# Latent attention's projections with tokens on partitions, woven between the mLSTM's panels, and the heads' gating moved into the attention

## The chip, the core and the metric
One core of a Trainium2 chip runs one program. It has a matrix engine (TensorE, PE below), a vector engine (DVE), a scalar engine (ACT), GpSimd (POOL) and a queue engine (SP) that here only issues weight loads. The metric is the time of one execution in device microseconds; the kernel before has a median of 2100.88 us over 3 runs (2096.22 to 2100.93).

## What is computed
Two transformer blocks follow one another over 512 tokens of width 1024. The change is in the second block's mixer, which the reference writes so:
```python
proj = h @ w_in
u, v_m, o_pre, i_pre, f_pre, c_q, c_kv, k_r = split(proj)
u_c = silu(causal_dwconv(u, conv_w, conv_b))
q_m, k_m = u_h @ wq_m, u_h @ wk_m            # per head, 128 -> 64
hm = mlstm_chunkwise(q_m, k_m, v_h, ig, fg)
y_m = sigmoid(o_pre) * rmsnorm(hm)
q_a = rmsnorm(c_q) @ w_uq                    # 4 heads x (128 + 64)
kv = rmsnorm(c_kv) @ w_ukv                   # 4 heads x (128 + 128)
q_rope = apply_rope(rmsnorm(q_a[rope part]), cos, sin); q_nope = rmsnorm(rest)
k_rope = apply_rope(rmsnorm(k_r), cos, sin); k_nope = rmsnorm(kv[first part])
o_a = causal_block_attention(q, k, v);  y_a = rmsnorm(o_a)
return concat([y_m, y_a]) @ w_out
```
A first MLP stands before it, and a cross attention over 256 memory rows and a second MLP behind it.

## The kernel before, in words
Activations lie with features on partitions: `h_hi`, `h_lo` hold the normalised input as a high and a low part, and each product with weights is three products of fp32r operands (high with high, low with high, high with low). Weights come in panels. SP loads panel n into one of two raw slots, POOL splits it into `w_hi` and `w_lo` (lines 2563 and 2568, four pieces each), and may begin when PE has finished panel n-2, because the split buffers too have two slots. PE multiplies panels in the order in which `Linear` objects are made. A block of 512 results goes into one of four PSUM banks (`banks[blk % 4]`); PE may start block n when block n-4 has been read (`acc_free`).

`pe_panel` (line 393) multiplies with features on the output's partitions; `pe_panel_tokens` (line 439) with tokens there, two token tiles in one bank. `mlstm_pe` takes the gates' panel `L_if`, the two panels of u, two of v and two of the output gate by tokens, and turns the gate rows on the way (line 1863). DVE convolves each block of u (`mlstm_conv_dve`), then computes the gates' rows with four partitions in use (lines 1978 to 1991) and the rope angles. ACT waits for the gates before it reads v. Then come the q and k products, and the four heads: a broadcast (line 1911), Exp on ACT, scores (line 1886), their weighting on DVE (line 2009), values (line 1897) and division (line 2022).

`latent_pe`, `latent_act` and `latent_dve` do the latent attention's preparation after that, with features on partitions. c_q is projected behind the heads and c_kv behind that. Every RMS norm needs a sum over partitions: ACT squares a block, PE forms the sums with one-column products (line 2132), ACT and DVE take roots and inverses, PE spreads them into rows (line 2143), DVE multiplies (line 2151). V is turned to tokens by PE (line 2187). Rope's swaps are ACT copies, its products for q DVE and, at the end, POOL (`rope_pool`, lines 2348 to 2351), which stands in POOL's queue behind the splits of the first two output panels. Then `attn_pe`, `attn_act` and `attn_dve` run 16 units (4 heads by 4 query tiles): scores (line 1339), the masked minimum (line 1418), Exp (line 1385), transposes (line 1349), copy (line 1393), values (line 1363), result (line 1429). The output projection follows, with its mLSTM half first.

Of the kernel before, what the change touches and what calls it, by code (L numbers as in the profile page):

```python
# [20 lines left out]
F32 = mybir.dt.float32  # L21
# [6 lines left out]
P = 128  # L28
# [31 lines left out]
def build_program(nc, io, out):  # L60
    ctx = ExitStack()
    with ctx:
# [31 lines left out]
        cols = sb("cols", [P, 584])  # L94
# [47 lines left out]
        for k in range(CONV2):  # L142
# [15 lines left out]
        col_at["qr"], col_at["kr"] = ncol, ncol + 1  # L158
        part_loads = [(64, ncol, io["qk_norm_q_2"][:, NOPE:A_QK].rearrange("o p -> p o")),
                      (64, ncol + 1, io["qk_norm_k_2"][:, NOPE:A_QK].rearrange("o p -> p o"))]  # L160
        ncol += 2
        inv = io["rope_inv"].rearrange("(p o) -> p o", o=1)
        col_at["inv"] = ncol
        part_loads += [(64, ncol, inv), (96, ncol, inv)]
        ncol += 1
        col_at["ib"], col_at["fb"] = ncol, ncol + 1
        part_loads += [(0, ncol, io["b_igate_2"].rearrange("o h -> h o")), (0, ncol + 1, io["b_fgate_2"].rearrange("o h -> h o"))]
# [13 lines left out]
        ncol += 64  # L181
        col_at["neg_sink"] = ncol
# [115 lines left out]
        L_if = Linear(1, DB, 132, [0, 4], lambda i: w_in2[:, :, IF0:IF0 + 132])  # L298
        L_m = [Linear(2, DB, 256, [0, 128], column_panels(w_in2, c0, 2)) for c0 in (0, 512, 1024)]
        L_qm = Linear(1, 4, 64, [], lambda i: io["wq_m_2"][0].rearrange("h p e -> p h e"))  # L300
        L_km = Linear(1, 4, 64, [], lambda i: io["wk_m_2"][0].rearrange("h p e -> p h e"))
        for L in (L_qm, L_km):
            L.nb = 4
            Linear.blocks += 4
        L_km.b0 = L_qm.b0 + 4
        L_cq = Linear(1, DB, 256, [0, 128], lambda i: w_in2[:, :, CQ0:CQ0 + 256])
        L_ckv = Linear(1, DB, 256, [64, 128], lambda i: w_in2[:, :, IN2 - 256:IN2])
        uq_offs = [o for h in range(A_HEADS) for o in (A_QK * h, A_QK * h + 64)]
        L_uq = Linear(1, 2, 768, uq_offs, lambda i: rows_of(io["w_uq_2"][0]))
        L_ukv = Linear(1, 1, 1024, [128 * j for j in range(8)], lambda i: rows_of(io["w_ukv_2"][0]))  # L310
# [13 lines left out]
        const_loaded = sem("const_loaded")  # L324
        const_made = sem("const_made")
# [15 lines left out]
        def last_block(panel):  # L341
            for L in Linear.made:
                if L.p0 <= panel < L.p0 + L.n:
                    if L in (L_uq, L_ukv):
                        return L_uq.b0 + 16
                    return L.b0 + (panel - L.p0 + 1) * L.nb
            raise ValueError(panel)
# [140 lines left out]
        def act_to_features(act, dst, d0, nb, gain, tiles, ring=banks[4:8]):  # L488
            for b in range(nb):
# [7 lines left out]
        def dve_to_features(dve, dst, d0, nb, gain, tiles, ring=banks[4:8]):  # L497
            for b in range(nb):
# [1152 lines left out]
        def mix_act(act):  # L1651
# [4 lines left out]
            act.dma_start(XAGAIN, x_in).then_inc(x_loaded, 16)  # L1656
            preload(act, ACT.Sqrt)
# [50 lines left out]
        def mlp_act(act, k):  # L1708
            for half in range(2):
# [16 lines left out]
                if half == 0 and k == 0:  # L1726
                    act_evac(act, L2, lambda b: YA[:, b, :])
                if half == 1 and k == 0:
# [6 lines left out]
        def mlp_dve(dve, k):  # L1735
            for half in range(2):
# [9 lines left out]
                for b in range(16):  # L1746
# [5 lines left out]
                    low(b)  # L1752
                if half or k:
# [23 lines left out]

        o = 0
        QM = A(o, 1024).rearrange("p (b s) -> p b s", b=2); o += 1024
        KM = A(o, 1024).rearrange("p (b s) -> p b s", b=2); o += 1024
        RING = [A(o, 512), A(o + 512, 512)]; o += 1024
        EW = A(o, 1280); o += 1280

        ROW = [r[0:4, :] for r in (a_free_hi[:, 12, :], a_free_hi[:, 15, :], EW[:, 0:512], A(o, 512), EW[:, 512:1024], A(0, 512), A(1024, 512))]
        o = 5120

# [918 lines left out]
```

## Time and profile before
| | |
|---|---|
| Median of 3 runs | 2100.88 us |
| The profiled execution's own time, and its span | 2111.39 us, 2109.7 us |
| PE busy in the span | 1988.1 us (94%) |
| POOL | 1543.9 us (73%) |
| DVE | 890.7 us (42%) |
| ACT | 654.3 us (31%) |
| Mean granted clock of PE | 0.957 |
| Chain that ended last | PE 77%, POOL 12%, DVE 6% |

### The profile page before, as it was taken

Reading aid. Unit: us, or ns where it says so; the run is one execution under the profiler, and the core shown is the slowest. Engines: PE = TensorE matmul, PEld = TensorE weight load, DVE = VectorE, ACT = ScalarE, POOL = GpSimd, SP = SyncE. Lnnn points to the kernel's source line nnn. Section 1 sums busy time; section 2 is a strip of 40 time slices with the busy share of each in tenths; the row PEclk is TensorE's granted clock in tenths of the full one; section 3 lists DMA queues with packets and bytes.
Section 4 is the critical chain, followed back from the end, with each engine's and each line's share of the span. In section 5 each row is a group of like instructions: output and inputs, shape, how many; then the busy total and the mean of one; then the engine's idle time right before and its main releaser. Section 6 shows DMA issues by size and latency. Waiting matters only on the chain.

```text
span 2109.7 us, 26714 instructions
## 1 busy us (share of the span) xinstructions
PE 1988.1 (94%) x9907; PEld 1664.1 (79%) x9907; DVE 890.7 (42%) x1703; ACT 654.3 (31%) x1216; POOL 1543.9 (73%) x1379
## 2 busy tenths in 40 slices
PE   6999999999999999889999989889898889999998
PEld 4888888887878888778888877868667777888887
DVE  4566767641025435274014227742444055402421
ACT  4466666542035661132012002432231142200200
POOL 7799989797844449789889888633609809988985
PEclk9999999999999999999999999987698899999999
DMA  6222222123332222313332332201102302333232
GB/s 216 81 61 61 61 60 61 60 60 100 90 99 73 61 79 84 116 60 100 100 98 88 94 89 63 66 26 60 40 1 80 101 20 80 100 100 100 89 96 74
DMA packets 212124, 166.01 MB, mean 79 GB/s; under 512 B 13439, under 2 KB 208322, under 8 KB 211635
## 3 DMA queue, kind: packets, MB, share of 16 engines
q1 hardware_dynamic: 207126, 147.61, 23.6%
q10 hardware_dynamic: 4892, 17.01, 2.3%
q8 instruction: 64, 1.05, 0.2%
q14 instruction: 42, 0.34, 0.1%
HBM read 161.43 MB, written 7.37 MB: 80 GB/s over the span
## 4 chain that ended last, share of the span: by engine, by line
PE 77%; POOL 12%; DVE 6%; issue 2%; ACT 2%; DMA 0%; DVEq 0%; SPq 0%; ACTq 0%; POOLq 0%
PE bank L393 55%; POOL w_lo L2568 5%; POOL w_hi L2563 4%; PE bank L439 4%; PE bank L1363 3%; PE bank L1339 3%; PE bank L412 2%; PE bank L2132 1%; PE bank L1349 1%; PE bank L2239 1%; POOL arena L1056 1%; PE bank L1038 1%; DVE arena L1816 1%; PE bank L1016 1%; PE bank L485 1%
## 5 line engine op out<-in xcount | busy, mean ns | idle before, releaser
L2563 POOL TENSOR_TENSOR w_hi<-w_raw,one 128x512 fp32r<-128x512 f32 (+2 forms) x520 | 532.8, 1055 | 492.8 <-PE bank L393 415.2
L2568 POOL TENSOR_TENSOR w_lo<-w_raw,w_hi 128x512 fp32r<-128x512 f32 (+2 forms) x600 | 742.7, 1269 | 34.6 <-ACT w_hi L1201 30.2
L393 PE MATMUL bank<-h_hi,w_hi 128*128 128x512 f32 (+1 forms) x1096 | 436.9, 399 | 15.5 <-POOL w_lo L2568 8.1
L393 PE MATMUL bank<-h_hi,w_lo 128*128 128x512 f32 (+1 forms) x1096 | 426.0, 389 | 0.0
L393 PE MATMUL bank<-h_lo,w_hi 128*128 128x512 f32 (+1 forms) x1096 | 424.8, 388 | 0.0
L393 PE MATMUL bank<-a_hi,w_hi 128*128 128x512 f32 x848 | 332.7, 392 | 11.2 <-POOL w_lo L2568 6.7
L393 PE MATMUL bank<-a_hi,w_lo 128*128 128x512 f32 x848 | 331.9, 391 | 0.0
L393 PE MATMUL bank<-a_lo,w_hi 128*128 128x512 f32 x848 | 331.6, 391 | 0.0
L393 PEld LDWEIGHTS bank<-h_hi,w_hi 128*128 128x128 f32 x1096 | 209.8, 191 | 57.3 <-POOL w_lo L2568 9.2
L393 PEld LDWEIGHTS bank<-h_hi,w_lo 128*128 128x128 f32 x1096 | 209.2, 191 | 42.6
L393 PEld LDWEIGHTS bank<-h_lo,w_hi 128*128 128x128 f32 x1096 | 210.1, 192 | 36.9
L393 PEld LDWEIGHTS bank<-a_hi,w_hi 128*128 128x128 f32 x848 | 160.6, 189 | 46.0 <-POOL w_lo L2568 7.6
L393 PEld LDWEIGHTS bank<-a_hi,w_lo 128*128 128x128 f32 x848 | 160.2, 189 | 33.8
L393 PEld LDWEIGHTS bank<-a_lo,w_hi 128*128 128x128 f32 x848 | 160.5, 189 | 33.1
L1742 DVE TENSOR_TENSOR a_lo<-arena,a_hi 128x512 fp32r<-128x512 f32 x64 | 80.4, 1256 | 158.0 <-ACT a_hi L1714 158.0
L1722 ACT ACTIVATE arena<-bank 128x512 f32<-128x512 f32 x64 | 38.1, 596 | 323.2 <-PE bank L393 315.0
L439 PE MATMUL bank<-w_hi,h_hi 128*128 128x256 f32 x384 | 111.3, 290 | 7.1 <-ACT arena L1844 6.6
L439 PE MATMUL bank<-w_lo,h_hi 128*128 128x256 f32 x384 | 109.7, 286 | 0.0
L439 PE MATMUL bank<-w_hi,h_lo 128*128 128x256 f32 x384 | 109.7, 286 | 0.0
L923 DVE SCALAR_TENSOR_TENSOR arena<-bank,cols,arena 128x510 f32<-128x510 f32 (+1 forms) x128 | 95.5, 748 | 4.8 <-ACT arena L907 1.4
L1750 DVE TENSOR_TENSOR arena<-arena,bank 128x512 f32<-128x512 f32 x64 | 43.2, 675 | 99.1 <-ACT arena L1722 92.4
L439 PEld LDWEIGHTS bank<-w_hi,h_hi 128*128 128x128 f32 x384 | 74.8, 195 | 7.8 <-issue 6.8
(387 smaller groups left out, 2924.6 us busy)
## 6 DMA issues: line engine op xcount, KB each, us to landing
w_raw<-in_w_in SPq DMA_DIRECT2D x32, 1024.0 KB, 5.3
w_raw<-in_w_ff SPq DMA_DIRECT2D x32, 1024.0 KB, 5.4
w_raw<-in_w_mlp_in SPq DMA_DIRECT2D x16, 1024.0 KB, 5.3
w_raw<-in_w_mlp_out SPq DMA_DIRECT2D x16, 1024.0 KB, 5.8
w_raw<-in_w_in SPq DMA_DIRECT2D x25, 512.0 KB, 4.3
w_raw<-in_w_ssd_out SPq DMA_DIRECT2D x8, 1024.0 KB, 5.6
bias_rows<-bias_row ACTq DMA_DIRECT2D x1, 4096.0 KB, 16.1
w_raw<-in_w_attn_out SPq DMA_DIRECT2D x4, 1024.0 KB, 5.3
```

What stands on the lines that cost most here:

```text
L393: mm = pe.matmul(bank[:, 0:ntok], a, b[:, koff + k, 0:ntok], start=(k == 0 and n == 0), stop=(k == L.kb - 1 and n == 2))
L412: mm = pe.matmul(banks[blk % 4][:], a, b[:, koff + k, :], start=(k == 0 and n == 0), stop=(k == L.kb - 1 and n == 2))
L439: mm = pe.matmul(banks[blk % 4][:, t * L.w:(t + 1) * L.w], a[:, k, tok], b, start=(k == 0 and n == 0), stop=(k == L.kb - 1 and n == 2))
L485: mm = pe.transpose(ring[b % len(ring)][:, t * P:(t + 1) * P], src[:, t, b * P:(b + 1) * P], ident[:])
L923: ins = dve.scalar_tensor_tensor(dst[:, lo:hi], src[:, lo + s:hi + s], colv(f"conv_w{k}", conv_column(g, b)), dst[:, lo:hi], ALU.mult, ALU ...
L1339: mm = pe.matmul(score_bank[n % 2][:, 0:w["n"]], qT, kT, start=(i == 0), stop=(i == len(w["q"]) - 1))
L1363: mm = pe.matmul(value_bank[:, 0:dv], mem[1][n % 2][:, j * P:(j + 1) * P], w["v"][j], start=(j == 0), stop=(j == nb - 1))
L1722: act.activation(RL[b % 2], acc(L1, b), ACT.Relu).then_inc(ml_relu, 1)
L1742: dve.tensor_tensor(a_lo[:, b, :], SQR[b % 2], a_hi[:, b, :].bitcast(F32), ALU.subtract).then_inc(ml_lo, 1)
L1750: dve_link(dve.tensor_tensor(RL[b % 2], RL[b % 2], NROW[:], ALU.mult))
L2563: pool.tensor_tensor(w_hi[:, slot, part], raw[:, slot, part], one[:].broadcast_to([P, n]), ALU.mult).then_inc(split_hi, 1)
L2568: ins = pool.tensor_tensor(w_lo[:, slot, part], raw[:, slot, part], w_hi[:, slot, part].bitcast(F32), ALU.subtract)
```

## The change
- Panels are reordered: u (2 panels), gates (one block; i in the first 64 columns, f in the next), c_q, c_kv with k_r (192 columns), q and k of the mLSTM in one panel of 128 columns per head, v (2), q up, gate panel, k and v up, gate panel. c_q, c_kv and the two up projections are now multiplied with tokens on partitions, so their norms are sums along the free axis (ACT's Square with a running sum, or DVE reductions), and their results are turned by transposes on PE (16 for c_q, c_kv and k_r, 40 for q and k). V needs none. The one-column sums and the spread rows of this stage go.
- Rope tables are made with tokens on partitions (128 columns in place of 512) during the first MLP; POOL multiplies the gains in (12 products), ahead of the third panel's split. Rotation is done by DVE. `rope_pool` goes.
- The conv's split of block b is issued after the conv of block b+1. q and k of the mLSTM are copied by ACT instead of DVE.
- The latent attention starts right behind the mLSTM heads. The gating of the heads' outputs by the output gate, their transposes and splits are hooks in its units.
- The load of the saved memory features is issued when the attention starts. Six small loads (gains, positions) are issued by ACT before the output projection of the first mixer.

```diff
-        L_if = Linear(1, DB, 132, [0, 4], lambda i: w_in2[:, :, IF0:IF0 + 132])
-        L_m = [Linear(2, DB, 256, [0, 128], column_panels(w_in2, c0, 2)) for c0 in (0, 512, 1024)]
...
+        L_u = Linear(2, DB, 256, [0, 128], column_panels(w_in2, 0, 2))
+        L_if = Linear(1, DB, P, [0], lambda i: [w_in2[:, :, c:c + 64] for c in (IF0, IF0 + M_HEADS)])
         L_cq = Linear(1, DB, 256, [0, 128], lambda i: w_in2[:, :, CQ0:CQ0 + 256])
+        L_ckv = Linear(1, DB, 192, [0, 64], lambda i: w_in2[:, :, CKV0:IN2])
+        L_qk = Linear(1, M_HEADS, P, [0] * M_HEADS, lambda i: [io[w][0].rearrange("h p e -> p h e") for w in ("wq_m_2", "wk_m_2")])
+        L_v = Linear(2, DB, 256, [0, 128], column_panels(w_in2, 512, 2))
+        L_uq = Linear(1, 2, 768, [0] * 2 * T, lambda i: rows_of(io["w_uq_2"][0]))
+        L_gate_m = [Linear(1, DB, 256, [0, 128], column_panels(w_in2, 1024, 1))]
+        L_ukv = Linear(1, 1, 1024, [0] * 2 * T, lambda i: rows_of(io["w_ukv_2"][0]))
+        L_gate_m.append(Linear(1, DB, 256, [0, 128], column_panels(w_in2, 1280, 1)))
...
         def mlstm_pe(pe):
+            pe_panel_rows(pe, L_u, 0, h_x, normed("mix2"))
+            pe_panel_with_root(pe, L_u, 1)
+            pe_panel(pe, L_if, 0, 0, h_x)
+            pe_panel_tokens(pe, L_cq, 0, 0, h_x)
+            pe_panel_tokens(pe, L_ckv, 0, 0, h_x)
+
+            pe.wait_ge(sp_lo, 4)
...
+            pe_panel_tokens(pe, L_v, 0, 0, h_x)
+            pe_panel_tokens(pe, L_v, 1, 1, h_x, only=0)
+            pe.wait_ge(lt["low"], 1)
...
+            pe_panel_tokens(pe, L_v, 1, 1, h_x, only=1)
...
+            for i in range(2 * T):
+                up_pe(pe, L_uq, i, 8, 384)
+            pe_panel_tokens(pe, L_gate_m[0], 0, 0, h_x)
+            pe.wait_ge(split_ready, L_ukv.p0 + 1)
+            for i in range(2 * T):
+                up_pe(pe, L_ukv, i, 10, 512)
+            pe.wait_ge(ml["act"], 4)
+            for f in range(6):
+                turn_pe(pe, f)
+            pe_panel_tokens(pe, L_gate_m[1], 0, 0, h_x)
+            for f in range(6, 10):
+                turn_pe(pe, f)
             mlstm_bc_pe(pe, 0)
...
+        def low_rank_act(act):
+
+            tokens_act(act, L_cq, 0, lambda t: CQT[:, t, :])
+            tokens_act(act, L_ckv, 0, lambda t: CKT[:, t, :])
...
+        def q_block_act(act, i):
+            t, j = i // 2, i % 2
+            bank = acc(L_uq, i, 0, P, 384)
+            act.wait_ge(acc_ready, L_uq.b0 + i + 1)
+            act.activation(QT[t][:, j * 384:(j + 1) * 384], bank, ACT.Copy)
+            if i >= 2:
+                act.wait_ge(lt["red"], i - 1)
+            act.activation(SQUARES[i % 2][:, 0:384], bank, ACT.Square).then_inc(acc_free, 1)
...
+        HEAD_AT = {"scale": 2, "turn": 4, "hi": 5, "lo": 6}
 
         def latent_pe(pe):
...
+            first = tp_n["pe"]
+            hooks = {HEAD_AT["turn"] + h: [lambda h=h: pe_to_features(pe, OM, T, h + 1, OM_RING, counted(ml["head"], 0), first=h)] for h in range(4)}
+            pe.wait_ge(ml["out"], 4 * M_HEADS)
+            attn_pe(pe, latent_units(), AMEM, hooks)
+            pe.wait_ge(tp_free, first + 4)
             for b in range(4):
                 pe_panel(pe, L_out2, b // 2, b // 2, a_x, only=b % 2, ks=range(0, 4))
...
-                if panel == L_out2.p0 + 2:
-                    rope_pool(pool)
```

## Rows read from the trace of the kernel before
**Rows 1.** The page: PE's line of section 1, clock in 40 slices.
```profile
PE 1988.1 (94%) x9907; PEld 1664.1 (79%) x9907; DVE 890.7 (42%) x1703; ACT 654.3 (31%) x1216; POOL 1543.9 (73%) x1379
...
PEclk9999999999999999999999999987698899999999
```
**Rows 2.** Table of stretches; columns in its first line.
```profile
core 0: us, PE busy (x) PEld busy (x) DVE busy (x) ACT busy (x) POOL busy (x), PEclk, DMA share, GB/s
...
1295.50:1364.00 68.50, 60.86 (x442) 58.15 (x440) 52.92 (x54) 17.34 (x29) 49.49 (x40) 0.95 0.22 66
1364.00:1410.20 46.20, 40.03 (x146) 27.35 (x144) 24.67 (x71) 20.64 (x66) 20.00 (x24) 0.78 0.16 52
...
1458.00:1486.00 28.00, 28.00 (x100) 23.80 (x99) 4.75 (x7) 3.60 (x8) 0.00 (x0) 0.51 0.00 1
...
1515.20:1537.00 21.80, 21.80 (x54) 10.25 (x54) 5.48 (x26) 5.83 (x18) 11.01 (x9) 0.61 0.03 9
1537.00:1561.70 24.70, 23.32 (x130) 15.36 (x130) 13.84 (x67) 11.78 (x31) 0.00 (x0) 1.00 0.00 0
```
**Rows 3.** Timeline, PE: start, us, instruction, [idle before, releaser].
```profile
1337.13 0.55 PE L439 MATMUL bank<-w_hi,h_hi 128*128 128x256 f32 x1 [6.63 <-ACT arena L1844]
...
1515.20 0.46 PE L1339 MATMUL bank<-a_free_lo,a_free_hi 128*128 128x128 f32 x2 [3.21 <-POOL arena L2351]
...
1561.74 0.47 PE L393 MATMUL bank<-a_hi,w_hi 128*128 128x512 f32 x1
```
**Rows 4.** Chain of work in time (start, us, what), and one timeline row, PE.
```profile
1352.44 11.70 PE bank L439 x96
...
1410.24 11.19 PE bank L393 x48
...
1572.76 1.91 PE L485 MATMUL bank<-ident,arena 128*128 128x128 f32 x16
```
**Rows 5.** Timeline, POOL: one split of a full panel.
```profile
1295.93 4.81 POOL L2563 TENSOR_TENSOR w_hi<-w_raw,one 128x512 fp32r<-128x512 f32 x4 [1.89 <-PE bank L393]
1300.70 6.38 POOL L2568 TENSOR_TENSOR w_lo<-w_raw,w_hi 128x512 fp32r<-128x512 f32 x4
```
**Rows 6.** Timeline, DVE: conv's start, the gate chain and two of its operations.
```profile
1296.24 0.69 DVE L1811 TENSOR_TENSOR a_free_hi<-bank,a_free_lo 128x512 f32<-128x512 f32 x1
...
1332.15 1.52 DVE L1978 SCALAR_TENSOR_TENSOR arena<-a_free_hi 4x512 f32<-4x512 f32 x1
...
1338.70 1.65 DVE L809 TENSOR_TENSOR arena<-arena 4x512 f32<-4x512 f32 x1
...
1343.76 0.68 DVE L811 TENSOR_TENSOR arena<-arena 4x512 f32<-4x512 f32 x1
...
1350.53 0.41 DVE L1991 TENSOR_SCALAR arena<-arena 4x512 f32<-4x512 f32 x1
```
**Rows 7.** Timeline, ACT: table load, first Exp of the heads, Square, copies.
```profile
1351.69 1.28 ACT L1847 ACT_TABLE_LOAD   x1
...
1370.08 0.40 ACT L1927 ACTIVATE arena<-a_free_lo,small 128x128 f32<-128x128 f32 x1
...
1382.21 0.29 ACT L1955 ACTIVATE a_free_lo<-arena 128x128 f32<-128x128 f32 x1
...
1448.81 1.08 ACT L2280 ACTIVATE arena<-bank 64x512 f32<-64x512 f32 x2
```
**Rows 8.** Timeline, PE and DVE: first score and last scaling of the heads.
```profile
1371.98 0.69 PE L1886 MATMUL bank<-arena 64*128 64x512 f32 x1 [1.10 <-DVE arena L2001]
...
1409.58 1.13 DVE L2022 TENSOR_SCALAR arena<-bank,small 128x128 f32<-128x128 f32 x4
```
**Rows 9.** Timeline, PE: scores of the attention at full clock.
```profile
1535.10 1.02 PE L1339 MATMUL bank<-a_free_lo,a_free_hi 128*128 128x512 f32 x2
...
1538.17 0.39 PE L1339 MATMUL bank<-a_free_lo,a_free_hi 128*128 128x128 f32 x2
...
1547.19 0.28 PE L1339 MATMUL bank<-a_free_lo,a_free_hi 128*128 128x128 f32 x1
```

More of the change, by code:

```diff
@@ L1752, in mlp_dve @@
                     low(b)
+                if half == 0 and k == 0:
+                    rope_tables_dve(dve)
                 if half or k:
@@ new lines, in turned_bank, with turn_pe @@
+        def turned_bank(f):
+            return banks[4 + f % 4] if f < 6 else banks[4 + (f - 6) % 3]
+        def turn_pe(pe, f):
+            if f >= 4:
+                pe.wait_ge(lt["kept"], 6 if 6 <= f < 9 else f - 2 if f == 9 else f - 3)
+            bank = turned_bank(f)
+            if f < 4:
+                pe.wait_ge(lt["qn"], f + 1)
+                parts = [(h * P, QT[f][:, h * A_QK:h * A_QK + NOPE]) for h in range(A_HEADS)]
+            elif f < 6:
+                first = 2 * (f - 4)
+                pe.wait_ge(lt["qn"], first + 2)
+                parts = [(c * 256 + n * P, RT[first + n][:, c * P:(c + 1) * P]) for c in range(2) for n in range(2)]
+            else:
+                pe.wait_ge(lt["kn"], f - 5)
+                parts = [(h * P, KT[f - 6][:, h * P:(h + 1) * P]) for h in range(A_HEADS)]
+            for c, part in parts:
+                mm = pe.transpose(bank[:, c:c + P], part, ident[:])
+            mm.then_inc(lt["turn"], 1)
@@ new lines, in turned_act @@
+        def turned_act(act, f):
+            act.wait_ge(lt["turn"], f + 1)
+            bank = turned_bank(f)
+            if 4 <= f < 6:
+                first = 256 * (f - 4)
+                act.activation(QR[:, :, first:first + 256], bank[:].rearrange("p (c s) -> p c s", c=2), ACT.Copy).then_inc(lt["kept"], 1)
+            else:
+                dst, gain, t = (QN, "qn", f) if f < 4 else (KN, "kn", f - 6)
+                act.activation(dst[:, :, t * P:(t + 1) * P], bank[:].rearrange("p (h f) -> p h f", h=A_HEADS), ACT.Copy,
+                               scale=colv(gain)).then_inc(lt["kept"], 1)
@@ new lines, in up_pe @@
+        def up_pe(pe, L, i, k0, width):
+            t, j = i // 2, i % 2
+            blk = L.b0 + i
+            tok = slice(t * P, (t + 1) * P)
+            pe.wait_ge(acc_free, blk - 3)
+            for k in range(L.kb):
+                c = k * L.w + j * width
+                wh, wl = (w[:, L.p0 % 2, c:c + width] for w in (w_hi, w_lo))
+                for n, (a, b) in enumerate(((a_hi, wh), (a_lo, wh), (a_hi, wl))):
+                    mm = pe.matmul(banks[blk % 4][:, 0:width], a[:, k0 + k, tok], b, start=(k == 0 and n == 0), stop=(k == L.kb - 1 and n == 2))
+            mm.then_inc(acc_ready, 1)
@@ L1898, in mlstm_pe @@
                     mm.then_inc(ml["num"], 1)
-            for b in range(2):
-                place = (L_cq.b0 + b) % 4
-                if place >= 2:
-                    pe.wait_ge(ml["out"], 4 * (M_HEADS - 1) + place - 1)
-                pe_panel(pe, L_cq, 0, 0, h_x, only=b)
-            pe_to_features(pe, OM, T, 4, OM_RING, counted(ml["head"], 0))
         def mlstm_bc_pe(pe, h):
```

810 lines of the change are left out of this document (377 added, 433 removed).

## The prediction

> **What bounds the kernel now.** I read the page's engine lines and its clock line first: PE is busy for 94% of the span, and the granted clock sinks only in the slices around 1265 to 1560 us [rows 1]. That stretch is the second block's mixer, all that the change touches; so I read the table of stretches for it next, then PE's timeline for what each pause waited for. The table shows a stage in two halves [rows 2]. From 1295.50 to 1364.00 PE works on the mLSTM's projections (60.86 of 68.50 us, clock 0.95). From 1364.00 to 1410.20 it does the mLSTM heads. Then, up to 1515.20, comes the latent attention's preparation, 105 us in which no other weights are multiplied: PE looks busy for all of 1458.00 to 1486.00, but at clock 0.51 and with 100 instructions, since blocks of three products alternate with one-column products that form sums of squares. Its end, the first score, waits 3.21 us for POOL's rope products, which stand behind two weight splits in POOL's queue [rows 3]. The attention follows from 1515.20 to 1561.74 [rows 3], its first half at clock 0.61 [rows 2]. So this is a chain of small steps over four engines rather than PE work, and it bounds the kernel.
>
> **The change, part by part.** Everything is added on PE's clock of the profiled execution. Up to 1295.50 nothing moves: the first panel by rows and the panel with the root stay 48 products each. (POOL now splits 2048 elements where the first panel had 1056, before its post-norm additions; by the row of a full split this is some 5 us more, in a queue that then waits for PE's last panel of the MLP anyway: taken as 0, at most +2.)
>
> 1. Gates: one block in place of two. A full block pair of 48 products takes 11.19 us [rows 4], so 24 take 5.6: to 1301.1. But a panel's split may only start when the panel two before it is done. The split of c_q starts at 1295.5 and takes 4.81 + 6.38 = 11.2 [rows 5]: PE waits until 1306.5. The 12 gain products on POOL fall before this, while the panel before is still multiplied.
> 2. c_q by tokens, 96 products of 256 columns: 11.70 at full clock [rows 4]. After the pause of 6.63 us in the old kernel such a panel ran from 1337.13 to 1351.3 [rows 3], 14.2 in all; I take 14.2: 1320.7.
> 3. c_kv and k_r by tokens, 96 products of 192 columns. No row has this width. The nearest are 256 columns (0.12 us each) and 128-column transposes (1.91 us for 16, also 0.12) [rows 4], so 11.6 us: 1332.3. The other bound is the attention's plain fp32, where a score of 512 columns is recorded as two passes, 1.02 us together [rows 9]: 192 columns would be 0.38, all 96 products 36, or +25. I stay with 0.12, between whose two rows the width lies.
> 4. The second c_kv block needs the gates' bank, which DVE frees after the conv. A conv period is 7.3 to 8 us without the 1.43 us wait for ACT, which the new order fills; DVE starts 2.4 earlier, having no gates ahead (1296.24 becomes 1293.8) [rows 6]. Conv ends at 1325, the gates are read at 1327, and the gate chain of 18.8 us (1332.15 to 1350.94) ends at 1346. This holds nothing at 1332.
> 5. q and k of the mLSTM, 12 products instead of 24: 2.8, plus about 0.7 of bank waits behind ACT: 1335.8. Then the next panel's split, started at 1332.3, is ready at 1342.8 or so. ACT is as late: after the gates (1332) it reads four blocks (3.3), takes 12 squares (4, by 0.29 for 128 columns), loads a table (1.28) and copies the first head (1.1, two of 0.54) [rows 7]: 1342.5. Wait 7 us; the panel again 14.2: 1357.
> 6. Half a panel 5.8, 16 transposes for c_q, c_kv and k_r with their wait 2.4, half a panel 5.8: 1371. ACT must then read the bank, load a table and take one Exp (0.84 + 1.28 + 0.63) before the rows are turned: 1374.
> 7. q up, 48 products of 384 columns, 8.4 us of PE. ACT copies and squares every block: by 0.29 for 128 columns and 0.54 for 512 [rows 7] about 0.5 a time, so 8 x 1.0, a table load of 1.3 and 8 roots of 0.2, 11 in all. To 1384.5. A gate panel 11.7: 1396.
> 8. k and v up, 24 products, 5.5 of PE; ACT reads each bank twice and DVE once, 0.85 a block. DVE comes from four norm-and-rotate groups. They take 12 us if two-tensor operations run as at 1343.76 (0.68 for 512 columns), 16 if as at 1338.70 (1.65), when POOL was splitting [rows 6]. With 8 pairs of sums, estimated at 0.7 as one pass over under 512 columns, it is free at 1394 or 1398. I take the later, since POOL is splitting then: 1405.
> 9. 24 transposes 3, gate panel 11.7, 16 transposes and the broadcast 3: 1422.7. ACT's last read, table load and four copies (0.6 each): first Exp of the heads at 1424.5.
> 10. Heads: they ran from the first Exp at 1370.08 [rows 7] to DVE's last scaling at 1409.58 + 1.13 [rows 8], 40.6 us. 1.9 of it passed before the first score at 1371.98 [rows 8], held by the copies of q and k, which are now long there: 38.7, to 1463.2.
> 11. Attention directly behind: as before 46.5 us. Gating the heads' outputs is now inside it: 16 transposes on PE (1.9 [rows 4]), 16 DVE products and 4 splits (some 7 us by 0.28 and 0.68 each, beside a DVE that is busy 13.84 of 24.70 [rows 2]); the first Exp waits for a root and a table load, some 3 us, under the first three units' scores. Taken +3: 1512.7.
>
> In step 8, DVE unhindered would end the sum at 1510.7 if nothing else were late by then. The Trainium skill (SBUF — State Buffer, Terms, the shared port pair) says that DVE and GpSimd take one port pair in turn, each for a whole instruction; by that rule it is 1512.7, and the two rows agree with it.
>
> The attention ended at 1561.74, so 49 us go: -105 between the heads and the attention, +53 in front of the heads, +3 inside the attention. What follows keeps its order and its waits. The memory's load is now issued at about 1464; allowing 10 us for it and 10 for its two POOL passes, the two output splits (2 x 11.2 [rows 5]) end by 1507, under the attention. Were they later, the output panels would be late by as much. Rope tables now run in the first MLP: 13 DVE operations of 128 columns, while DVE waits for the second product, and three Sin with table loads on ACT (3.5 us) before a block that PE ends 5.6 us later: 0. Six more DMA issues on ACT precede the reading of the output projection, whose first block is 11 us away: 0 unless an issue takes over 1.8; at most +3.
>
> The profiled execution (2111.39, span 2109.7) becomes 2062; it stands 10.5 above the median of 2100.88. The median becomes 2052.
>
> **Rivals.** (A) Narrow products run at the plain rate: +25 of step 3, no cover: 2077. For: no row of that width. Against: 128-column rows are not slower than 256. (B) The clock holds: heads and attention do not follow pauses of 3 to 4 us and short products any more. The attention's first two heads took 23 us against 9.02 for one later [rows 9], so 5 more there; the heads ran at 0.78 [rows 2], another 8 if at 1.0: 2039. Against: heads ran slow in spite of a busy start. (C) Small hand-overs that I haven't seen, a microsecond at each of some 25 new waits among ACT, DVE and PE: 2077 too. (D) Slower: PE's clock stays at half through the new stretch. Its PE work from 1295.5 to 1424.5 is about 100 us at full clock (the sum above without its waits), and half the clock doubles it; some 15 us of waits would vanish under it, so the cost is up to 85 and the time 2137. It decides from about 55 us of such work. For it: 1458 to 1486 shows recorded-busy PE at 0.51. Against: the panels there followed one-column products; after the 6.63 us pause the clock was back within one panel. (E) The change doesn't overlap what it means to: in steps 7 and 8 DVE's 22 us and ACT's 18 come after PE's work and not beside it, +38, 2090.
>
> The Trainium skill (TensorE: Matmul & The Clock Gate, Part 4) says that transposes don't count as busy for the clock. That is a rule for D, since 56 transposes now lie between panels; the row of 16 transposes at full clock [rows 4] and the panel after it in a stretch of mean 0.94 speak against its mattering for runs of 2 to 3 us.
>
> **How the numbers follow.** Forecast (2044 to 2062) 0.50; B 0.15; A 0.10; C 0.15; D 0.05; E 0.05. The range leaves out D, E and the tail of B: 2035 to 2078. A difference of 0.3% (6 us) is what a measurement can tell. Faster: all but D and the slow end of E, 0.93; same 0.02; slower 0.05.
>
> **What would show it.** In the profile of the changed kernel: PE pauses of about 5 and 7 us ahead of c_q and of the mLSTM's v panel, released by POOL's split; products of 192 columns spaced 0.12 us (A: 0.3 or more); no one-column products up to the attention; first Exp of the heads near 1425; nothing but one unit's latency between the last head and the first score; attention in 45 to 50 us with DVE below 90% busy; granted clock at 1.0 through the q, k and gate panels (D: 0.5); and the output panels waiting no longer than before. It is wrong if the first Exp comes after 1440, or if the attention takes over 55.

## The result, and the profile after

The kernel after takes 2070.74 us (median of 4 runs, 2068.83 to 2073.17) against 2099.82 us for the kernel before on the same chip (4 runs, 2096.22 to 2100.93). The ratio is 0.9865, 95% interval 0.9848 to 0.9882: 29 us or 1.4% faster, where 49 us were forecast. 2070.74 lies inside the range, 19 us above the forecast of 2052.

One thing is needed to read these numbers: the kernel before does not take the same time in every execution (2089 to 2113 us), and its profiled execution was one of the long ones. The profiled execution of the kernel after (2070.29, span 2068.6) lies at its median. So the pair of profiles differs by 41 us and the medians by 29.

The page of the kernel after, PE's line and the granted clock (before: [rows 1]):

```profile
PE 1939.5 (94%) x9759; PEld 1626.9 (79%) x9759; DVE 910.5 (44%) x1732; ACT 673.0 (33%) x1285; POOL 1531.3 (74%) x1367
...
PEclk9999999999999999989999998897698899999999
```

PE's timeline of the kernel after: start, us, instruction, and the idle time before it with what ended it (before: [rows 3]).

```profile
1303.91 0.58 PE L434 MATMUL bank<-w_hi,h_hi 128*128 128x256 f32 x1 [6.55 <-POOL w_lo L2591]
...
1341.59 0.58 PE L434 MATMUL bank<-w_hi,h_hi 128*128 128x256 f32 x1 [10.76 <-POOL w_lo L2591]
...
1371.19 0.63 PE L2124 MATMUL bank<-ident,arena 4*128 4x4 f32 x8 [2.96 <-ACT arena L2211]
...
1400.11 0.80 PE L2088 MATMUL bank<-w_hi,a_hi 128*128 128x512 f32 x1 [3.95 <-DVE a_free_lo L2024]
...
1421.75 0.44 PE L2064 MATMUL bank<-ident,a_free_hi 128*128 128x128 f32 x2 [1.71 <-ACT a_free_lo L2075]
...
1464.44 1.06 PE L1334 MATMUL bank<-a_free_lo,a_free_hi 128*128 128x128 f32 x3 [2.02 <-DVE arena L2285]
...
1520.97 0.48 PE L388 MATMUL bank<-a_hi,w_hi 128*128 128x512 f32 x1
```

The two pauses that the prediction named are there, ahead of c_q (6.55 us) and of the v panel (10.76), both released by POOL's split, and three shorter ones, for ACT (2.96 and 1.71) and for DVE (3.95), are there too. The heads end and the first score of the latent attention follows 2.02 us later, at 1464.44; the attention ends at 1520.97. The stage begins at 1265.41, so it takes 255.6 us, of which 199.0 in front of the first score and 56.5 in the attention. In the kernel before it was 292.5, 245.9 and 46.5 [rows 3].

The table of stretches of the kernel after, from the heads on (before: [rows 2]).

```profile
core 0: us, PE busy (x) PEld busy (x) DVE busy (x) ACT busy (x) POOL busy (x), PEclk, DMA share, GB/s
...
1422.30:1464.40 42.10, 37.36 (x122) 24.56 (x120) 19.12 (x64) 16.64 (x61) 0.00 (x0) 0.68 0.00 0
1464.40:1475.10 10.70, 10.66 (x16) 3.79 (x16) 5.93 (x13) 4.01 (x13) 5.21 (x2) 0.52 0.28 99
1475.10:1486.70 11.60, 8.50 (x30) 6.08 (x30) 11.49 (x16) 2.81 (x8) 11.60 (x9) 0.50 0.00 0
1486.70:1497.40 10.70, 9.51 (x37) 5.54 (x36) 8.86 (x21) 3.46 (x9) 9.85 (x9) 0.75 0.30 98
1497.40:1520.90 23.50, 22.12 (x122) 14.28 (x121) 14.38 (x66) 12.06 (x31) 0.00 (x0) 1.00 0.14 46
```

The attention's first two heads (1464.4 to 1497.4) took 33 us, where the kernel before needed 23 (1515.20 to 1538.17 [rows 3, 9]). In their middle DVE is busy for 11.49 of 11.60 us, and so is POOL, while PE, at half clock (1.2 GHz), has 3 us to spare. From 1497.4 on the stage runs much as it did before (23.5 us, clock 1.00). What DVE and POOL do there, and in front of the v panel, on their timelines (before: [rows 5, 6]):

```profile
1328.00 0.68 DVE L806 TENSOR_TENSOR arena<-arena 4x512 f32<-4x512 f32 x1
1328.71 1.41 DVE L807 TENSOR_TENSOR arena<-arena 4x512 f32<-4x512 f32 x1
...
1342.21 3.79 DVE L1969 TENSOR_SCALAR arena<-arena,latent_stats 128x256 f32<-128x256 f32 x4
...
1471.69 8.54 DVE L2294 SCALAR_TENSOR_TENSOR arena<-arena,small 128x128 f32<-128x128 f32 x4
1480.16 0.68 DVE L1413 CUSTOM_DVE_ANT_0 a_free_lo<-bank,cmask 128x512 f32<-128x512 f32 x1
```

```profile
1328.21 5.71 POOL L2586 TENSOR_TENSOR w_hi<-w_raw,one 128x512 fp32r<-128x512 f32 x4 [6.75 <-PE bank L434]
1333.88 7.65 POOL L2591 TENSOR_TENSOR w_lo<-w_raw,w_hi 128x512 fp32r<-128x512 f32 x4
...
1469.81 3.60 POOL L2371 TENSOR_TENSOR h_hi<-arena,one 128x2048 fp32r<-128x2048 f32 x1 [66.48 <-DMA arena<-mem_features_saved]
1473.49 4.51 POOL L2373 TENSOR_TENSOR h_lo<-arena,h_hi 128x2048 fp32r<-128x2048 f32 x1
```

Four gating products (L2294) take 8.54 us, from the end of POOL's first pass over the memory, through the second, into the first piece of a split. Operations that read a bank (L1413) keep their 0.68. POOL loses as well: the v panel's split takes 13.3 us beside the gate chain, where one beside little DVE work takes 9.0 (pool_first, 1416.95 to 1425.89).

### The profile page after: what moved, and what is told of

It is laid out like the page before. It is cut to its first block, busy times and chain, and to the rows that moved or that the text cites. A ratio compares the mean times of both kernels' runs of the same rounds, so it can differ in the third digit from the quotient of the medians.

```text
span 2068.6 us, 26459 instructions
## 1 busy us (share of the span) xinstructions
PE 1939.5 (94%) x9759; PEld 1626.9 (79%) x9759; DVE 910.5 (44%) x1732; ACT 673.0 (33%) x1285; POOL 1531.3 (74%) x1367
## 4 chain that ended last, share of the span: by engine, by line
PE 78%; POOL 13%; DVE 5%; issue 2%; ACT 1%; DMA 0%; DVEq 0%; SPq 0%; ACTq 0%; POOLq 0%
PE bank L388 55%; PE bank L434 6%; POOL w_lo L2591 5%; POOL w_hi L2586 4%; PE bank L1358 3%; PE bank L1334 2%; PE bank L407 2%; POOL x_features L671 1%; PE bank L1344 1%; POOL arena L1051 1%; PE bank L1033 1%; PE bank L1011 1%; PE bank L480 1%; PE bank L2164 1%; DVE arena L576 1%
## 5 line engine op out<-in xcount | busy, mean ns | idle before, releaser
L2586 POOL TENSOR_TENSOR w_hi<-w_raw,one 128x512 fp32r<-128x512 f32 (+3 forms) x516 | 531.3, 1060 | 398.0 <-PE bank L388 351.4
L388 PE MATMUL bank<-h_hi,w_hi 128*128 128x512 f32 (+1 forms) x1056 | 420.4, 398 | 14.7 <-POOL w_lo L2591 8.5
L388 PE MATMUL bank<-h_hi,w_lo 128*128 128x512 f32 (+1 forms) x1056 | 409.7, 388 | 0.0
L388 PE MATMUL bank<-h_lo,w_hi 128*128 128x512 f32 (+1 forms) x1056 | 409.2, 387 | 0.0
L388 PEld LDWEIGHTS bank<-h_hi,w_hi 128*128 128x128 f32 x1056 | 201.9, 191 | 54.4 <-POOL w_lo L2591 9.9
L434 PE MATMUL bank<-w_hi,h_hi 128*128 128x256 f32 (+1 forms) x448 | 129.7, 290 | 17.3 <-POOL w_lo L2591 17.3
L434 PE MATMUL bank<-w_hi,h_lo 128*128 128x256 f32 (+1 forms) x448 | 128.0, 286 | 0.0
L434 PE MATMUL bank<-w_lo,h_hi 128*128 128x256 f32 (+1 forms) x448 | 127.9, 286 | 0.0
L434 PEld LDWEIGHTS bank<-w_hi,h_hi 128*128 128x128 f32 x448 | 87.6, 195 | 18.2 <-POOL w_lo L2591 18.1
L434 PEld LDWEIGHTS bank<-w_hi,h_lo 128*128 128x128 f32 x448 | 87.6, 196 | 0.0
```

Source lines behind the costliest of these rows:

```text
L388: mm = pe.matmul(bank[:, 0:ntok], a, b[:, koff + k, 0:ntok], start=(k == 0 and n == 0), stop=(k == L.kb - 1 and n == 2))
L434: mm = pe.matmul(banks[blk % 4][:, t * L.w:(t + 1) * L.w], a[:, k, tok], b, start=(k == 0 and n == 0), stop=(k == L.kb - 1 and n == 2))
L2586: pool.tensor_tensor(w_hi[:, slot, part], raw[:, slot, part], one[:].broadcast_to([P, n]), ALU.mult).then_inc(split_hi, 1)
```

## The experiments

Two numbers are read from each profile: the time from the stage's first product to the first score, and the attention's own, up to the first product of the output projection (the expectations below read it to the end of the last weighted sum, 0.25 us later: 50.35 and 47.96 there are 50.1 and 47.7 here). In warm_heads and warm_attn the attention is counted from the products added in front of it. With the medians, and their ratio to the kernel before on the same chip:

| kernel | to the first score | attention | median, us | ratio (95% interval) |
|---|---|---|---|---|
| before, as profiled | 245.9 | 46.5 | 2099.8 | |
| before_again, before_third, before_fourth | 245.9, 233.7, 235.4 | 48.2 each | one execution each: 2109.6, 2095.2, 2097.5 | |
| after | 199.0 | 56.5 | 2070.7 | 0.9865 (0.9848 to 0.9882) |
| pool_first | 199.1 | 50.1 | 2063.7 | 0.9842 (0.9790 to 0.9893) |
| hooks_late | 199.1 | 54.0 | 2067.9 | 0.9863 (0.9812 to 0.9915) |
| both | 199.2 | 51.9 | 2067.8 | 0.9859 (0.9807 to 0.9910) |
| mem_early | 200.5 | 47.7 | 2064.5 | 0.9838 (0.9788 to 0.9888) |
| warm_heads | 200.1 | 55.2 | 2070.9 | 0.9868 (0.9817 to 0.9919) |
| warm_attn | 200.5 | 47.8 | 2064.3 | 0.9823 (0.9789 to 0.9857) |
| merged | 195.7 | 57.1 | 2066.7 | 0.9828 (0.9766 to 0.9890) |
| best | 191.6 | 46.7 | 2055.4 | 0.9775 (0.9750 to 0.9800) |
| best_low_first | 191.7 | 46.7 | 2051.3 | 0.9776 (0.9748 to 0.9804) |

The chips differ by up to 4.4 us in the kernel before, and only the last two intervals lie clear of that of the kernel after. What the other edits do is therefore read from the two stretches of their profiles, one profile each, and not from the medians.

### Where the profiled execution of before lost 12 us: before_again, before_third, before_fourth

The kernel before, unchanged, three more times.

> The kernel before, profiled once more. Its profiled execution lay 10.5 us above its median, and the kernel after's at its own. If those 10.5 us are chance in the stretch that the change touches (from the first mLSTM panel to the last weighted sum of the latent attention: 292.5 us then), this profile has it at 280 to 287, with the time nearer the median. If the chance lies elsewhere, the stretch is again 290 to 294 and the other stretches are shorter.

> The kernel before, profiled a third time. Both profiles so far had a mean granted clock of 0.956 to 0.957 and 2109.6 and 2111.4 us; unprofiled executions had 0.956 (2109.9), 0.963 to 0.966 (2096 to 2100) and 0.968 (2089). If the time follows the clock that a given execution gets, a third profile has one of these pairs; one near 2098 would show in which stretch it is faster, which I expect to be 1364 to 1515 us (the heads and the latent preparation), by about 10 us. If the profile itself costs the 10 us, it is again near 2110.

> The kernel before, profiled a fourth time. From the stage's start to the first score of the latent attention it took 245.9, 245.9 and 233.7 us in the three profiles so far, with times of 2111.4, 2109.6 and 2095.2. If TensorE's clock in the old preparation is a draw of its own in each execution, this one has 233 to 246 us there and a time that lies within 3 us of 2095 plus what it has over 233.7. If it is not, the time and the stretch are not tied together.

Each kernel's timeline, first product of the stage and first score of the attention: before_again, then before_third, then before_fourth.

```profile
1266.66 0.76 PE L412 MATMUL bank<-h_hi,w_hi 128*128 128x512 f32 x1 [6.17 <-DVE h_lo L647]
...
1512.53 0.46 PE L1339 MATMUL bank<-a_free_lo,a_free_hi 128*128 128x128 f32 x2 [3.13 <-POOL arena L2351]
```

```profile
1264.00 0.76 PE L412 MATMUL bank<-h_hi,w_hi 128*128 128x512 f32 x1 [5.36 <-DVE h_lo L647]
...
1497.67 0.46 PE L1339 MATMUL bank<-a_free_lo,a_free_hi 128*128 128x128 f32 x2 [2.85 <-POOL arena L2351]
```

```profile
1265.03 0.76 PE L412 MATMUL bank<-h_hi,w_hi 128*128 128x512 f32 x1 [6.17 <-DVE h_lo L647]
...
1500.42 0.46 PE L1339 MATMUL bank<-a_free_lo,a_free_hi 128*128 128x128 f32 x2 [3.12 <-POOL arena L2351]
```

The stretch with one-column products between blocks, from its first to its last product, in the table of stretches (PE alone) of the kernel before as first profiled and then of before_third:

```profile
1454.80:1493.40 38.60, 36.82 (x152) 0.64 0.00 0
```

```profile
1449.00:1475.90 26.90, 24.29 (x153) 1.00 0.00 1
```

The same instructions took 38.6 us at a mean clock of 0.64 in both long executions and 26.9 us at 1.00 and 0.99 in the two short ones, 11.7 us less, and the way to the first score is 245.9 us in both long ones and 233.7 and 235.4 in the others. The fourth expectation held: 2097.51 is 2.3 us above 2095.2, the stretch 1.7 longer. The first one (280 to 287 in the stage) failed, 294.0: it met the long form again, and it is the third that settled it. So 10.5 to 12.2 us of the stage that the change replaced were there only in some executions, the profiled one among them. In front of the stage the same four executions differ as well: it starts between 1264.0 and 1269.3 us.

### The attention's 10 us: pool_first, hooks_late, both

pool_first:

```diff
-                if panel == L_out2.p0:
+                if panel == L_out2.p0 + 2:
                     memory_pool(pool)
```

> The kernel after, with POOL's two memory passes behind the splits of the output projection's first two panels instead of in front of them. Those splits then run beside the mLSTM heads, when POOL is idle, and no longer beside the attention's first two heads (33.0 us of 56.5). Theory 1 (DVE, 99% busy in 1475 to 1487 of the kernel after, is slowed there by POOL): the attention takes 51 to 53 us, the time falls by 4 to 5. Rival (TensorE's clock of 0.5, left by the heads' short products, sets the pace and DVE only looks full): 55.5 to 56.5 us, no change of time.

hooks_late (both: this and the edit above):

```diff
-        HEAD_AT = {"scale": 2, "turn": 4, "hi": 5, "lo": 6}
+        HEAD_AT = {"scale": 9, "turn": 11, "hi": 12, "lo": 13}
```

> The kernel after, with the gating, turning and splitting of the mLSTM heads' outputs seven units later in the attention (units 9 to 16 in place of 2 to 9). Theory 1 (the added operations meet POOL's splits on a full DVE): these units run at full clock and without POOL, the attention takes 51 to 53 us. Rival, clock: 55 to 57 us, as the first two heads stay at 30 us or more. Second rival: the added operations cost the same wherever they are, since DVE is busy for 90% in a steady head: 56 us with the first two heads at 25 and the last two at 31.

> Both edits: memory passes behind the two output splits, and the gating seven units later. Theory 1: nothing disturbs DVE in the first two heads, so the attention takes 47 to 49 us as in the kernel before plus 1 to 3 for the added operations; the time falls by 7 to 9 us, to about 2062. Rival, clock: 54 us or more, and under 2 us gained. If each edit alone takes the whole excess, both together give no more than one.

pool_first took 50.1 us in the attention, 6.4 less than the kernel after and a little more gain than expected; its median is 7 us lower, which the intervals do not separate. What was left is on its timelines, DVE's and then POOL's:

```profile
1466.77 1.14 DVE L2294 SCALAR_TENSOR_TENSOR arena<-arena,small 128x128 f32<-128x128 f32 x4
...
1469.77 7.03 DVE L2294 SCALAR_TENSOR_TENSOR arena<-arena,small 128x128 f32<-128x128 f32 x4
```

```profile
1467.95 3.60 POOL L2371 TENSOR_TENSOR h_hi<-arena,one 128x2048 fp32r<-128x2048 f32 x1 [42.06 <-DMA arena<-mem_features_saved]
1471.62 4.50 POOL L2373 TENSOR_TENSOR h_lo<-arena,h_hi 128x2048 fp32r<-128x2048 f32 x1
```

Four products alone: 1.14 us. The same four beside the two passes: 7.03, ending 0.7 us after the second pass (1476.12). The Trainium skill says this of such pairs (SBUF — State Buffer, Who interferes with whom): a DVE instruction with both inputs in SBUF and a GpSimd instruction that reads SBUF exclude each other for a whole instruction; one with a single SBUF input, outside its two-port modes, is free. The trace agrees: L2294 waits, and L1413, with one input in a bank, does not.

The later gating did less: 54.0 us alone, where 51 to 53 were expected, and 51.9 together with POOL's new order, where 47 to 49 were expected and pool_first alone has 50.1. Two rows of the tables of stretches show why, hooks_late and then both:

```profile
1463.00:1475.00 12.00, 12.00 (x21) 4.83 (x21) 2.12 (x9) 4.61 (x13) 6.89 (x2) 0.50 0.25 87
```

```profile
1497.00:1516.50 19.50, 18.15 (x107) 12.31 (x106) 15.65 (x63) 10.40 (x27) 0.00 (x0) 1.00 0.00 1
```

With no gating in it the attention's start has PE busy for 12.00 of 12.00 us at half clock and DVE for 2.12: PE paces it, and DVE has room. At its end the clock is 1.00 and DVE, with the gating, is busy for 15.65 of 19.50. So the gating stands where it costs least as the change has it, and the second rival (same cost wherever) is closer than theory 1, which had counted on DVE's room at the end. The attention's first two heads say it by themselves: 33.0 us in the kernel after, with gating and POOL's splits; 26.5 in pool_first, with gating and no splits; 26.1 in hooks_late, with splits and no gating; 26.1 in both, with neither. It takes the two together to cost 6 to 7 us.

### POOL out of the attention altogether: mem_early

The memory is loaded into the normed rows' buffer, free since the last gate panel, and split there in place, and POOL's order is that of pool_first (not shown again):

```diff
             tokens_act(act, L_gate_m[1], 0, lambda t: OM[:, t, 256:512], ACT.Sigmoid)
+            act.dma_start(h_lo[:, :, 0:N_MEM].bitcast(F32), mem_dram.ap().rearrange("p (b s) -> p b s", b=DB)).then_inc(mem_loaded, 16)
...
-            act.dma_start(MEMB, mem_dram.ap()).then_inc(mem_loaded, 16)
...
-            memory = MEMB.rearrange("p (b s) -> p b s", b=DB)
+            memory = h_lo[:, :, 0:N_MEM].bitcast(F32)
```

> The kernel after, with the memory loaded into the normed rows' own buffer (free from the last gate panel at 1418.6 on) and split there in place by POOL, behind the two output splits: splits and memory passes all run beside the mLSTM heads, none beside the attention. With only the passes left there (the run with POOL's order changed) the attention took 50.35 us, and four DVE products took 7.03 us in it, against 1.14 for the next four, while POOL made the passes. Theory 1 (DVE waits for POOL's long passes): these 5.9 us go in part, attention 46 to 48 us, time 2059 to 2062. Rival: DVE's wait there is covered by TensorE at half clock, attention stays at 49.5 to 50.5 us. Second rival: the heads, now beside the passes, take longer by what the attention gains.

The attention took 47.7 us, as in the kernel before with no gating in it (46.5 to 48.2): gating adds nothing that shows there when POOL is away. Of the 2.4 us that came off pool_first's attention some may be the clock's: its mean was 0.51 in pool_first and 0.50 here over the first 15.5 us, but 0.80 and 0.98 over the next 13, and no run separates the two. The heads took 1.4 more, so the second rival had a part, and the median did not follow (2064.5 against 2063.7; 2059 to 2062 were expected). On mem_early's timelines, DVE's row and POOL's:

```profile
1434.47 1.43 DVE L2282 SCALAR_TENSOR_TENSOR small<-small 128x4 f32<-128x4 f32 x1
1435.93 0.17 DVE L2283 TENSOR_TENSOR small<-small 128x4 f32<-128x4 f32 x1
```

```profile
1431.36 4.52 POOL L2373 TENSOR_TENSOR h_lo<-h_lo,h_hi 128x2048 fp32r<-128x2048 f32 x1
```

A product of four columns, 0.16 us elsewhere (1434.56 in the kernel after), ends when the pass does.

### Does the half clock cost time: warm_heads, warm_attn

```diff
+        def warm_pe(pe, bank, n=1):
+            for _ in range(n):
+                pe.matmul(bank[:], m_lt[:], h_hi[:, 0:2, 256:512], start=True, stop=True)
```

warm_heads, on the kernel after, calls it ahead of the heads' last transposes (8), ahead of most waits in each head (1) and at the attention's units 0 to 6 (2). warm_attn, on mem_early, has those of the attention alone.

> The kernel after, with products whose result nobody reads: 8 of 512 columns in the wait of 1.7 us ahead of the mLSTM heads, 6 to 7 in each head, 2 at each of the attention's first 7 units. They tell whether the low clock in heads (0.50 to 0.93, TensorE recorded busy for all of 1426 to 1434 at 0.50) and in the attention's first two heads (0.50) costs time. Theory, clock: the plain fp32 products do not hold the clock, these do; the heads take 32 to 36 us in place of 42, the attention's first two heads 25 to 28 in place of 33, time 2055 to 2062. Rival: the clock stays at half whatever is added, and the products cost their 10 to 15 us: time 2078 to 2085. Second rival: the clock rises but DVE and ACT bind: within 3 us of the kernel after.

> The kernel with the memory split early (attention 47.96 us, 0 us of POOL work in it, clock 0.50 to 0.70 in its first 21 us), and two products of 512 columns whose result nobody reads in front of each of the attention's first 7 units. With products added in heads and attention of the kernel after, the clock was 1.00 in 1464 to 1475, but DVE then waited for POOL and nothing was gained; here POOL is away. Theory, clock: the first two heads are paced by TensorE at half clock, the attention takes 42 to 45 us, time 2059 to 2062. Rival: DVE and ACT pace it, or the added products cost what the clock gives: 47 to 49 us, time 2064 to 2066.

Neither gained: 2070.9 and 2064.3, the kernels without the products 2070.7 and 2064.5. The rows of 1464 to 1486 of warm_heads, and of 1475 to 1486 of warm_attn and mem_early:

```profile
1464.00:1475.00 11.00, 10.61 (x41) 5.93 (x41) 7.83 (x13) 4.19 (x14) 5.47 (x2) 1.00 0.29 96
1475.00:1486.00 11.00, 4.63 (x14) 2.96 (x15) 10.89 (x16) 2.34 (x7) 11.00 (x9) 0.59 0.00 0
```

```profile
1475.00:1486.00 11.00, 11.00 (x60) 7.10 (x60) 7.53 (x31) 5.49 (x15) 0.00 (x0) 1.00 0.00 1
```

```profile
1475.00:1486.00 11.00, 11.00 (x44) 7.05 (x45) 6.41 (x26) 3.99 (x11) 0.00 (x0) 0.70 0.00 0
```

The clock did rise, to 1.00 where it had been 0.52. In warm_heads PE then stood idle for 6.4 of 11 us behind a DVE busy for 10.89 beside POOL: in the kernel after, the clock is hardly what its attention waits for (55.2 us in place of 56.5). In its heads the mean clock rose from 0.67 to 0.84 (1422 to 1464) and the first score came no earlier. In warm_attn PE stays full, and the added products cost what the clock gave. A low clock has a price all the same, seen in best, where the heads' second half ran at 1.00 (table of stretches: 0.53 up to 1444.5, 1.00 from there). Its broadcast and its 20 weighted sums in the slow part and at full clock:

```profile
1438.56 2.07 PE L2190 MATMUL bank<-arena,ident 4*128 4x512 f32 x2
1440.56 4.05 PE L2181 MATMUL bank<-arena,a_free_hi 128*128 128x129 f32 x20
...
1448.11 1.12 PE L2190 MATMUL bank<-arena,ident 4*128 4x512 f32 x2
1449.16 2.50 PE L2181 MATMUL bank<-arena 128*128 128x129 f32 x20
```

From a head's first score to the next head's is 10.25 us in the kernel after (1444.53 to 1454.78) and 7.05 here (1444.54 to 1451.59), at a mean clock of 0.67 and of 1.00: the lower clock costs 3.2 us in this head.

### The pause ahead of the v panel: merged, best, best_low_first

merged puts the weights of c_kv and of q and k into one panel of 2048 elements, so that the v panel's split starts when c_q is done:

```diff
-        L_ckv = Linear(1, DB, 192, [0, 64], lambda i: w_in2[:, :, CKV0:IN2])
-        L_qk = Linear(1, M_HEADS, P, [0] * M_HEADS, lambda i: [io[w][0].rearrange("h p e -> p h e") for w in ("wq_m_2", "wk_m_2")])
+        L_ckv = Linear(1, DB, 192, [0, 64] + [0] * M_HEADS, None)
+        L_ckv.size, QK0 = DB * 192 + M_HEADS * P, DB * 192
...
+        L_qk = Blocks()
+        L_qk.b0, L_qk.p0 = L_ckv.b0 + 2, L_ckv.p0
```

> The kernel after, with the weights of c_kv and of the mLSTM's q and k in one panel of 2048 elements in place of two (1536 and 512), so that the split of the v panel starts when c_q is done and not when c_kv is. Theory: the wait of 10.76 us ahead of the v panel goes whole, with 1 to 2.5 us of slow clock behind it; the norm chain on DVE (last rotated keys at 1353) is then late by 0 to 3 us at the transposes: first Exp of the heads 8 to 12 us earlier than 1424.3, time 2059 to 2063. Rival: the merged split, 11 us instead of 8.4, is late for c_kv, and the wait moves there: 2 to 4 us gained. Second rival: DVE's chain is the bound and only 3 to 5 us are gained.

PE's row and ACT's of merged:

```profile
1337.63 0.55 PE L440 MATMUL bank<-w_hi,h_hi 128*128 128x256 f32 x1 [5.72 <-ACT arena L2208]
```

```profile
1336.89 0.59 ACT L2208 ACTIVATE arena<-bank 64x512 f32<-64x512 f32 x1
```

POOL's part of the wait went; ACT's was right behind, at 1337.6, 71 us after the stage's start. The gain is 3.3 us to the first score, not 8 to 12. The attention, untouched, stayed at 57.1. (One of its four executions took 2053.64 us, the others 2065.33 to 2070.59; why is not known.) best takes this and mem_early (its passes in eight pieces), and on ACT puts the squares of c_q ahead of c_kv's copies and the copies of q and k (now a function, qk_act) ahead of c_kv's squares:

```diff
+                if c == 0:
+                    act.wait_ge(acc_free, L_cq.b0 + 2)
+                if c == 4:
+                    tokens_act(act, L_ckv, 0, lambda t: CKT[:, t, :])
+                    act.wait_ge(acc_free, L_ckv.b0 + 2)
+                    qk_act(act)
                 for t in range(T):
...
+            for b in range(0, DB, 2):
+                pool.tensor_tensor(h_hi[:, b:b + 2, 0:N_MEM], memory[:, b:b + 2, :], one[:].unsqueeze(2).broadcast_to([P, 2, N_MEM]), ALU.mult).then_inc(mem_hi, 1)
```

> Early memory split, in eight passes of 512 elements in place of two of 2048, with the merged c_kv and q/k panel, and on ACT the copies of the mLSTM's q and k in front of c_kv's squares and the squares of c_q in front of c_kv's copies. In the run with the merged panel alone the wait ahead of the v panel was 5.72 us, for ACT's copies of q and k, which stood behind 12 squares and a table load (4.05 + 1.28 + 0.67 us). Theory 1 (three mechanisms, each as sized by its own run): this wait goes down to under 2 us; the transposes then wait for DVE's norm chain, up to 3 us; first score 6 to 8 us earlier than 199.0 us after the stage's start; attention 48 us in place of 56.5; the heads lose no 1.3 us to a pass any more, as none is longer than 1.2 us: time 2053 to 2057. Rival (what is taken away in front comes back at DVE's chain, which ends at 1353 whatever PE does): first score 3.4 us earlier as with the merged panel alone, time 2058 to 2061.

It has 191.6 and 46.7 us, and 2055.44 us (6 runs, 2052.41 to 2056.40): ratio 0.9775 to the kernel before, interval 0.975 to 0.980, against 0.9848 to 0.9882 for the kernel after. Theory 1 held for the pause (between c_q and the transposes PE waits 1.11 us for ACT and 1.26 for POOL, and then 2.09 for DVE) and for the attention. It failed for the heads: a score in their first half, beside POOL's pieces, waited 1.46 us for DVE in place of 0.92.

best_low_first lets DVE scale c_q and c_kv ahead of the gates' two scans, and turns the rotated keys after the v panel:

```diff
             gates_dve(dve)
             low_rank_dve(dve)
+            gate_sums_dve(dve)
+            key_rope_dve(dve)
```

> The best kernel so far (2055.44 us), with DVE scaling c_q and c_kv in front of the mLSTM gates' two scans and not behind them, and the rotated keys turned after the v panel's second half. There the transposes waited 2.09 us for DVE (L1988), whose chain from the gates to c_kv's scaling ended 88.3 us after the stage's start, in the kernel after at 85.5 to 87.7. Theory (DVE's chain is what bounds the stretch in front of the transposes): the 2.09 us go and nothing else is late, first score 189 to 190 us after the stage's start in place of 191.6, time 2053 to 2054. Rival (the scans come back as a later wait, for the row transposes or for the copies that ACT now makes later): first score unchanged at 191 to 192, time 2055 to 2056.

The row transposes came 4.7 us earlier than in best (95.1 us after the stage's start, 99.8 there), but the first score did not (191.7), since in this profile the clock was 0.65 over the heads' second half, where best had 1.00. The median, 2051.27, is 4.2 us below best's, but the kernel before was faster by as much on that chip: the ratios are 0.9776 (0.9748 to 0.9804) and 0.9775. Whether this edit gains anything stays open. On its timelines, a four-column product of DVE again, and POOL's pass in pieces of 512:

```profile
1426.29 2.24 DVE L2301 SCALAR_TENSOR_TENSOR small<-small 128x4 f32<-128x4 f32 x1
```

```profile
1423.58 4.93 POOL L2394 TENSOR_TENSOR h_lo<-h_lo,h_hi 128x512 fp32r<-128x512 f32 x4
```

## Why the prediction was right and wrong

Right in sign, in mechanism and in nearly all of its places; too large by 20 us. The steps that failed are 11, the gating's +3 us inside the attention, and the last line, which took 10.5 us off the forecast for the median. By the prediction's own steps, each counted from the stage's start (1269.28 there, 1265.41 in the kernel after):

| step | forecast | measured |
|---|---|---|
| 1, c_q starts | 37.2 | 38.5 |
| 3, c_kv ends | 63.0 | 62.5 |
| 5, v panel starts | 73.5 | 76.2 |
| 7, gate panel ends | 126.7 | 127.9 |
| 8, k and v up end | 135.7 | 139.0 |
| 9, first Exp of the heads | 155.2 | 158.9 |
| 10, first score | 193.9 | 199.0 |
| 11, attention ends | 243.4 | 255.6 |

- Step 11 is the one that failed inside the sum: +3 us was given for the gating inside the attention, measured +8 to +10 (56.5 against 48.2 and 46.5). The text summed DVE's own 7 us by uncontended rows against DVE's busy share of the later heads, and placed the memory's passes and the output splits "under the attention" at no cost. PE's queue did not wait for them, but DVE did. pool_first and mem_early show the term without the splits and without both: 50.1 and 47.7 us, around the forecast's 49.5. Nothing needed to be unknown here: the row of a slowed DVE operation [rows 6] had been used for step 8 and was not applied to step 11.
- Step 5: a pause of 7 us was forecast, 10.76 measured. The split was taken at 10.5 us, but beside the gate chain it took 13.3. That ACT would be as late (1342.5) was right to within two microseconds: merged took POOL's part away and found ACT at 71.1 us after the start, where 73.2 had been forecast.
- Step 8: +2.1, DVE's norms beside POOL's split; PE waited 3.95 us for them. Here the slower row had been taken, and it was still a little short.
- Step 3: rival A is refuted. 96 products of 192 columns and 96 of 256 took 24.0 us together, and those of 192 columns followed each other by 0.11 us (1317.74 to 1318.63).
- Step 10: 40.1 us in place of 38.7, at a mean clock of 0.68; the 3.2 us that one head lost by the lower clock (from best, above) show how much of this step is the clock.
- The last line of the sum was the other half of the miss: "The median becomes 2052", by the 10.5 us by which the profiled execution lay above it. These were not spread over the whole: they lay in the very stretch that the change removes. Against a short execution of the kernel before (before_third, 281.8 us for the stage), the change gains 26.2 us, near the 29 of the medians. The forecast for the profiled pair, 2062, should have been the forecast for the median too.

So of the 20 us that are missing from the gain, 10.7 were never there to be had (292.5 against 281.8), 7.0 are the attention and 5.1 small steps in front of it; some 2.8 the other way lie outside the stage and are not traced, less than its start varies. Of the rivals, C (small hand-overs) has its mechanism in the 5.1 but not its size (25 us, 2077). Rival B's time for the attention did not come: the clock was 0.50 to 0.75 in its first two heads. Rival D's half clock did not come in the new stretch (0.86 to 0.94 up to the heads), nor did E's missing overlap: steps 7 and 8 took 32.7 us (1371.75 to 1404.44) where 31 were forecast, not 38 more. Of the two signs by which it was to be wrong, the first Exp came in time (1424.3) but the attention took over 55, so by its own sign it was wrong there: the text had the right alarm and the wrong term. DVE stayed below 90% over the whole attention (40.7 of 56.5 us), as was said, but was 99% busy in 1475.1 to 1486.7: the sign was a mean and hid the stretch that decides. The clock of 1.0 was there in the gate panel (1381.7 to 1393.3) but not around it (0.83 in q up, 0.85 in k and v up).

## What to carry to other kernels

Before work is put "under" another stage, list for that stretch not only whether its engine is idle but which other engine's operations it slows: here POOL's splits beside DVE's SBUF-only operations cost 6.4 us (after against pool_first). When the profiled execution is longer than the median, profile again before the difference is subtracted: if it lies in the stretch that the change replaces, it is part of the gain that isn't there. And where two waits end within a microsecond or two of each other, removing one buys only the distance to the next (10.76 became 5.72); both have to go.

## What the runs showed of the hardware

- DVE operations with their inputs in SBUF and POOL's operations take turns by whole instructions, and size does not protect the small one: 0.16 us became 1.43 and 2.24. Cutting the passes into pieces of 1.2 us did not bound the wait: the 2.24 us reach past the end of one piece (1427.29) to the end of the next (1428.51). POOL's own split took 8.97 us across the start of the heads (pool_first), where DVE reads banks, and 13.3 beside the gate chain.
- TensorE's granted clock for one instruction stream is not fixed: the same 152 or 153 recorded products had 0.64, 0.64, 1.00 and 0.99 in four executions of one kernel and took 38.6, 38.6, 26.9 and 26.9 us; the heads' second half had 1.00 and 15.2 us in best, 0.65 and 20.6 us in best_low_first. PE was recorded busy throughout at 0.50 from 1426 to 1434 of the kernel after, with plain fp32 products. What decides between the levels there stays open.
